# Six gate pairs by seven products instead of four, the first pair loaded and summed ahead of its stage, and the order of the vector work before it

## The reference, cut to what matters

```python
h = x @ p['w_in'][l]
fa, fb, fm = split_cols(h, [A_COLS, B_COLS, 2 * D_MODEL])
...
o_b = o_b.reshape(bsz, t, D_B).astype(x.dtype) * jax.nn.silu(z_b)
g_a, g_b = split_cols(fm, [D_MODEL, D_MODEL])
merged = jax.nn.sigmoid(g_a) * (o_a @ p['w_up_a'][l]) + jax.nn.sigmoid(g_b) * (o_b @ p['w_up_b'][l])
y = layer_norm(ALPHA * x + merged @ p['w_out'][l], p['ln_g'][l], p['ln_b'][l])
```

## Time and profile before

| | us |
|---|---|
| median of 3 runs | 2148.93 |
| lowest and highest of them | 2145.84, 2149.21 |
| profiled execution, its own time | 2150.8 |
| its span from the first to the last instruction | 2149.1 |
| PE busy | 2109.5 (98%) |
| DVE busy | 1081.9 (50%) |
| POOL, ACT busy | 511.9, 411.4 |

### The profile page before, as it was taken

How to read it: one execution, slowest core, us unless ns; L and a number is a source line. 1 busy time by engine, 2 the same in 40 slices (tenths; PEclk the granted TensorE clock), 3 DMA queues, 4 the chain that set the end, 5 groups by cost and what they waited for, 6 DMA issues and landing times.

```text
span 2149.1 us, 48889 instructions
## 1 busy us (share of the span) xinstructions
PE 2109.5 (98%) x21468; PEld 1861.7 (87%) x21468; DVE 1081.9 (50%) x1885; ACT 411.4 (19%) x1168; POOL 511.9 (24%) x380
## 2 busy tenths in 40 slices
PE   9999999999999999999999999999999999999997
PEld 8999977777887779999999999777777877899996
DVE  3454344443725523674575443555547165247745
ACT  1111111122113511110121121222221043111002
POOL 3433300002011123333324333000020112134333
PEclk9999999999999999999999999999999999999998
DMA  8445333335643365555354453332365334645551
GB/s 305 169 160 171 118 133 101 101 101 201 218 138 104 109 228 184 162 167 177 128 182 163 157 172 123 110 101 101 101 218 191 119 118 144 217 170 165 172 170 66
DMA packets 89124, 329.51 MB, mean 153 GB/s; under 512 B 11920, under 2 KB 11936, under 8 KB 86608
## 3 DMA queue, kind: packets, MB, share of 16 engines
q1 hardware_dynamic: 74736, 268.60, 37.1%
q0 software_dynamic: 11872, 53.59, 7.1%
q10 hardware_dynamic: 2304, 4.20, 0.6%
HBM read 315.91 MB, written 18.82 MB: 156 GB/s over the span
## 4 chain that ended last, share of the span: by engine, by line
PE 94%; DVE 4%; DMA 1%; issue 1%; ACT 0%; POOL 0%; SPq 0%; ACTq 0%; POOLq 0%; DVEq 0%
PE PB L805 28%; PE PB L853 3%; PE PB L884 3%; PE PB L880 3%; PE PB L875 3%; PE PB L868 3%; PE PB L864 3%; PE PB L858 3%; PE PB L1288 3%; PE PB L940 1%; PE PB L1022 1%; PE PB L1005 1%; PE PB L1007 1%; PE PB L1000 1%; PE PB L996 1%; PE PB L969 1%
## 5 line engine op out<-in xcount | busy, mean ns | idle before, releaser
L805 PE MATMUL PB<-XT,WT 128*128 128x264 f32 (+1 forms) x2816 | 691.3, 395 | 0.0
L805 PEld LDWEIGHTS PB<-XT,WT 128*128 128x128 f32 (+1 forms) x2816 | 508.5, 189 | 100.4 <-issue 15.2
L1494 ACT ACTIVATE VT<-PB 128x132 f32<-128x132 f32 (+2 forms) x280 | 79.3, 292 | 581.4 <-PE PB L868 130.6
L1494 ACT ACTIVATE ARENA<-PB 128x128 f32<-128x128 f32 (+7 forms) x187 | 76.4, 429 | 261.5 <-PE PB L1187 65.6
L631 POOL DMA_DIRECT2D out<-in_c_win x16 | 8.1, 507 | 460.2 <-DVE ARENA L2113 460.2
L631 POOL DMA_DIRECT2D ARENA<-in_c_sel x64 | 40.0, 625 | 231.2 <-issue 231.2
L652 POOL TENSOR_TENSOR TOEP<-WT 128x1024 f32<-128x1024 f32 x20 | 47.2, 2360 | 172.8 <-PE PB L868 167.8
L652 POOL TENSOR_TENSOR TOEP<-H 128x1024 f32<-128x1024 f32 x20 | 48.2, 2410 | 141.6 <-PE PB L868 137.0
L868 PE MATMUL PB<-ARENA,TOEP 128*128 128x132 f32 x640 | 78.5, 276 | 0.0
L875 PE MATMUL PB<-ARENA,TOEP 128*128 128x132 f32 x640 | 78.5, 276 | 0.0
L884 PE MATMUL PB<-XT,TOEP 128*128 128x132 f32 x640 | 78.5, 276 | 0.0
(11 more groups left out here) (480 smaller groups left out, 4204.4 us busy)
## 6 DMA issues: line engine op xcount, KB each, us to landing
WT<-in_w_all SPq DMA_DIRECT2D x340, 512.0 KB, 4.4
H<-in_w_all SPq DMA_DIRECT2D x120, 512.0 KB, 4.4
KNVC<-in_w_all SPq DMA_DIRECT2D x40, 512.0 KB, 3.9
out<-in_c_win POOLq DMA_DIRECT2D x16, 512.0 KB, 5.3
ARENA<-in_c_cmp POOLq DMA_DIRECT2D x64, 128.0 KB, 4.4
ARENA<-in_c_sel POOLq DMA_DIRECT2D x64, 128.0 KB, 4.0
TOEP<-in_toep POOLq DMA_DIRECT2D x2, 2048.0 KB, 8.6
ARENA<-in_states POOLq DMA_DIRECT2D x4, 1024.0 KB, 11.2
```

Source lines behind the costliest of these rows:

```text
L805: ins = mm(PB[rows, bank, 0:T], WT[:, s, k, 0:rows.stop - rows.start], x, start=start, stop=stop)
L1494: return act(out, in_, ACT.Copy)
```

## The change

Four of the `ga` tiles per layer move from the table of tiles to the pairs: `TILES` has 42 entries and there are six gate pairs. The units behind the second scores go from 36 to 20; one unit is left under `gates`. The four blocks of the first gate pair go to buffers that are free early (the place of the k columns and of the first keys and values in H, and the second half of KNVC), and SP issues their loads ahead of tiles 35, 36, 40 and 37. POOL's first two sums wait for the scaled probabilities (`as_v ps`) instead of `zb_v out`. DVE makes t1 to t4 and OS2 directly behind the value product (`as_t o`), then `back`, OS4 and the z_B products.

```diff
+LAST_GA = 4
-         + [("zb", ZB0 + i) for i in range(8)] + [("gb", i) for i in range(16)] + [("ga", i) for i in range(8)])
+         + [("zb", ZB0 + i) for i in range(8)] + [("gb", i) for i in range(16)] + [("ga", i) for i in range(LAST_GA)])
-GATES, UPS, PAIRS = 4, 8, 8
+GATES, UPS, PAIRS = (16 - LAST_GA) // 2, 8, 8
+FIRST_AT = (35, 36, 40, 37)
-BEHIND_MIX.update({"as0": 12, "as1": 36, "as2": 6, "as3": 3})
+BEHIND_MIX.update({"as0": 12, "as1": 20, "as2": 6, "as3": 3})
...
+        old_keys, old_values = flat(H[:, K0:K0 + 8, :]), flat(H[:, KV0 + 2:KV0 + 6, :])
+        PW_FIRST = [block_of(old_keys, 0), block_of(old_keys, BLK * P), block_of(old_values, 0), PW[0][3]]
+        pair_blocks = lambda g: PW[g % 2] if g else PW_FIRST
...
+            def load_first(L, b):
+                if b == 0:
+                    sp.wait_ge(*step("gn_v", L, "out"))
+                if b == 2:
+                    sp.wait_ge(*step("as_v", L, "q"))
+                    sp.wait_ge(st_kv, 16 * (L + 1))
+                if b == 3:
+                    sp.wait_ge(*step("cm_v", L * 2 + 1, "out"))
+                load_block(L, 0, b)
+
             def load_pairs(L):
-                sp.wait_ge(*step("zb_v", L, "out"))
-                for b in (0, 2, 1, 3):
-                    load_block(L, 0, b)
                 for b in range(4):
                     sp.wait_ge(tile_done[b // 2], (L + 1) * N_TILES // 2)
                     load_block(L, 1, b)
-                for g in range(2, GATES + 2):
+                sp.wait_ge(*step("zb_v", L, "out"))
+                for b in (0, 2, 1, 3):
+                    pair_loaded(sp, L, 0, b)
+                    if b == 3:
+                        sp.wait_ge(*step("gp_t", L * GATES, "st4p"))
+                    load_block(L, 2, b)
+                for g in range(3, GATES + 2):
...
                 elif i > 3:
+                    if i in FIRST_AT:
+                        load_first(L, FIRST_AT.index(i))
                     sp.wait_ge(tile_done[s], u)
...
-                po.wait_ge(*step("zb_v", L, "out"))
+                po.wait_ge(*step("as_v", L, "ps"))
                 pair_loaded(po, L, 0, 0)
                 pair_loaded(po, L, 0, 2)
-                mark("os_p", L * BOTH, add(OS3, PW[0][0], PW[0][2], ALU.subtract), "s3")
+                mark("os_p", L * BOTH, add(OS3, PW_FIRST[0], PW_FIRST[2], ALU.subtract), "s3")
...
-                own("as_t", "tr")
-                for g in range(NG):
...
+                own("as_t", "o")
                 low, high = XT[:, 0:BLK, :], XT[:, BLK:KT, :]
...
                 second_sum(0)
+                own("as_t", "tr")
+                for g in range(NG):
...
+                mark("as_v", L, ins, "back")
                 fourth_sum(0)
+                own("zb_a", "tanh")
+                mark("zb_v", L, stt(TZB[:, :, :], TZB[:, :, :], 1.0, H[:, ZB0:ZB0 + 8, :], ALU.add, ALU.mult), "sz")
+                own("as_v", "back")
+                own("zb_v", "sz")
+                mark("zb_v", L, stt(H[:, ZB0:ZB0 + 8, :], H[:, Q0:Q0 + 8, :], 0.5, TZB[:, :, :], ALU.mult, ALU.mult), "out")
```

More of the change, by code:

```diff
@@ L81 @@
 LAST_ODD, EVENS = MAINS - 1 - MAINS % 2, (MAINS + 1) // 2
-PAIRED = [("ga", i) for i in range(8, 16)] + [("up", i // 2 + i % 2 * 8) for i in range(16)] + [("out", i) for i in range(16)]
-GATES, UPS, PAIRS = 4, 8, 8
+PAIRED = [("ga", i) for i in range(LAST_GA, 16)] + [("up", i // 2 + i % 2 * 8) for i in range(16)] + [("out", i) for i in range(16)]
+GATES, UPS, PAIRS = (16 - LAST_GA) // 2, 8, 8
 OUTS = GATES + UPS
@@ L307, in hybrid_trunk @@
         fresh()
-        TZB = take(P, 8, T)
+        TZB, OS = take(P, 8, T), take(P, 256)
         used[0] = slot
@@ L314, in hybrid_trunk @@
         PTZ = take(P, 4 * NB, 32).rearrange("p (i b) n -> p i b n", b=NB)
-        PCZ, PNT, OS = take(P, NB, 32), take(NB, 2, P), take(P, 256)
+        PCZ, PNT = take(P, NB, 32), take(NB, 2, P)
         assert used[0] <= at_att
@@ L509, in load_block @@
                 done = w_in_slot[b // 2][b % 2] if g % 2 else w_in_pair[b]
-                sp.dma_start(PW[g % 2][b], w_all[L, N_TILES + 2 * MAINS + 2 * g + b // 2, :, BLK * (b % 2):BLK * (b % 2) + BLK, :]).then_inc(done, 16)
+                sp.dma_start(pair_blocks(g)[b], w_all[L, N_TILES + 2 * MAINS + 2 * g + b // 2, :, BLK * (b % 2):BLK * (b % 2) + BLK, :]).then_inc(done, 16)
             def load_main(L, m, b):
@@ L737, in _ @@
                             dma(SVS[odd][:, m, pg, :].rearrange("p (a n) -> p a n", n=P), c_sel[L, page, :, 2:4, :], d_att[odd])
-                po.wait_ge(*step("zb_v", L, "out"))
+                po.wait_ge(*step("as_v", L, "ps"))
                 pair_loaded(po, L, 0, 0)
                 pair_loaded(po, L, 0, 2)
-                mark("os_p", L * BOTH, add(OS3, PW[0][0], PW[0][2], ALU.subtract), "s3")
+                mark("os_p", L * BOTH, add(OS3, PW_FIRST[0], PW_FIRST[2], ALU.subtract), "s3")
                 pair_loaded(po, L, 0, 3)
-                mark("os_p", L * BOTH, add(OS1, PW[0][2], PW[0][3], ALU.add), "s1")
+                mark("os_p", L * BOTH, add(OS1, PW_FIRST[2], PW_FIRST[3], ALU.add), "s1")
                 for g in range(1, BOTH):
@@ L890, in gate_pair @@
                 t0, t1 = slice(0, HALF), slice(HALF, T)
-                w = PW[g % 2]
+                w = pair_blocks(g)
                 first, second = PB[:, 2 + g % 2 * 2, :], PB[:, 3 + g % 2 * 2, :]
@@ L1448, in _ @@
                     elif g:
-                        all_projected(pe, L, "ga", 7)
+                        all_projected(pe, L, "ga", LAST_GA - 1)
                     up_pair(L, g)
@@ L1771, in _ @@
                     sc.wait_ge(*step("gp_v", it, "fin"))
-                    gate = H[:, 8 + 2 * g:10 + 2 * g, :].rearrange("p t n -> p (t n)")
+                    gate = H[:, LAST_GA + 2 * g:LAST_GA + 2 + 2 * g, :].rearrange("p t n -> p (t n)")
                     mark("gp_a", it, act(gate, f, ACT.Tanh, scale=0.5), "tanh")
@@ L2361, in second_sum @@
                     else:
-                        ins = tt(OS2, OS1, PW[g % 2][0], ALU.subtract)
+                        ins = tt(OS2, OS1, pair_blocks(g)[0], ALU.subtract)
                     mark("os_v", L * BOTH + g, ins, "s2")
@@ L2373, in fourth_sum @@
                     else:
-                        ins = tt(OS4, PW[g % 2][1], OS2, ALU.subtract)
+                        ins = tt(OS4, pair_blocks(g)[1], OS2, ALU.subtract)
                     mark("os_v", L * BOTH + g, ins, "s4")
+                own("as_t", "o")
                 low, high = XT[:, 0:BLK, :], XT[:, BLK:KT, :]
@@ L2385, in _ @@
                 second_sum(0)
-                fourth_sum(0)
+                own("as_t", "tr")
+                for g in range(NG):
+                    rows = slice((g % 2) * HD, (g % 2) * HD + HD)
+                    o = PB[rows, 0, (g // 2) * P:(g // 2) * P + P].rearrange("p (b h) -> p b h", h=NH)
+                    ins = cp(hq(g), o[:, :, 4 * g:4 * g + 4].rearrange("p b r -> p r b"))
+                mark("as_v", L, ins, "back")
+                fourth_sum(0)
+                own("zb_a", "tanh")
[3 more added lines that the diff above has]
+                mark("zb_v", L, stt(H[:, ZB0:ZB0 + 8, :], H[:, Q0:Q0 + 8, :], 0.5, TZB[:, :, :], ALU.mult, ALU.mult), "out")
                 def up_tokens(h):
@@ L2462, in _ @@
                     if g == 0:
-                        all_projected(ve, L, "ga", 7)
+                        all_projected(ve, L, "ga", LAST_GA - 1)
                         ve.wait_ge(*step("gp_a", (L + 1) * GATES - 1, "tanh"))
```

## The result

The changed kernel takes 2164.03 us (median of 7 runs, 2161.73 to 2172.26), the kernel before 2149.21 us beside it (7 runs, 2145.84 to 2156.03). The ratio is 1.0061, with an interval of 1.0049 to 1.0074: slower by 13 us (the medians alone lie 14.8 apart). The forecast was 2151.2 us within 2143.5 to 2155.5, so the time lies 8.5 us above the upper end. The profiled executions say the same: the span went from 2149.1 to 2162.4 us, 13.3 more.

The account below looks back on a forecast made before the run. TensorE, busy 98% of the span, was taken to bound the kernel. Per layer -28.6 + 25.2 + 3.8 = +0.4, for both +0.8, plus 1.5 for the clock: +2.3 on 2148.93 gives 2151.2 us, range 2143.5 to 2155.5.

Parts of the forecast that it names:

- Work of PE: Both layers: 64 units fewer against two more gate pairs, so PE's own work falls 3.4 us a layer, 6.8 in all.
- The place of the wait: At the first gate pair's fifth product, line 936, PE waits for VectorE's small addition, line 2441, in each layer.
- The size of the wait: At the first gate pair's fifth product: addition done after 13.25 us, PE there after 9.4, so 3.8 us a layer.
- T0: The end of the samples' value product, 785.41 before the change; the prediction counts PE's and VectorE's times from it.
- The clock: Behind the two waits of 3.8 us: one fall to half clock expected, +1.5 us, between 0 and +3.4.
- The rival on the clock: Behind the waits the clock falls in both layers: waits of 4.1, two half-clock stretches, +4.8 us, 2153.7; chance 0.20.
- signs of being wrong: Line 936 waiting under 2 us, tile 40 or values over a microsecond, or half clock past one stretch a layer.
- The values: Second half of the values: cover down to some 0.4 us, so a slightly later landing makes PE wait 0 to 0.5.
- the scaled probabilities: Line 805, behind the second scores: 20 units end at 768.3, probabilities finished at 764.99; no wait, 3.3 us to spare.
- tile 40: Its first half lands near 756.4, just when PE needs it; wait taken as 0, up to 1 us.
- the pairs behind the first: Gate stage: six gate pairs 12.60 us apart, but for the first.
- The range: Whole kernel: from 2143.5 us, where the wait is merely shorter, to 2155.5, for clock and loads together.

## Why the prediction was wrong

- **Work of PE (-6.8 us): right.** The stretch that holds the change is 6.7 us shorter where nothing waits in it. With at most 0.2 us of waiting left in each gate stage the kernel gains 5.8 us by the medians, and 3.2 to 9.3 by the interval of the ratio (0.15% to 0.43% of 2151.4).
- **The place of the wait: right.** Line 936 waits for line 2441 in both layers, and the two z_B products run right before it.
- **The size of the wait: the step that failed.** The sum of VectorE's instructions from T0 on took "the two large products for z_B, 2.46 and 2.28" from the earlier trace rows, where GpSimd stood idle beside them. In the new order product 4 of the same pair releases GpSimd's sums for pair 1 in the middle of the two products, and the second takes 4.31. The wait is 5.8 instead of 3.8 in each layer, 4.0 us in all; held back, the sums leave 3.86. The prediction looked at GpSimd's first two sums alone, and did not ask where those for pair 1 would fall. The trace of before could have hinted at it: the 128x132 sum of line 2427 takes 0.59 us at 818.33, while a GpSimd sum runs from 816.41 to 818.76; the same form takes 0.28 at its shortest (line 1948).
- The Trainium skill, "SBUF — State Buffer", section "Who interferes with whom", states that only the port pair which VectorE shares with GpSimd causes contention, as an exclusive lock; that a VectorE instruction with two inputs in SBUF contends with a GpSimd instruction that reads SBUF, and one with at most one such input, outside the two-port modes, does not; and that the order of issue decides which one blocks. The trace agrees: the four ends above are 2.20 and 2.21 apart, one instruction at a time, and the addition with one input in PSUM took its usual 0.29 beside a GpSimd sum.
- **The clock (+1.5 us for one fall): too small.** It fell in both layers, for 6.8 us each, and cost 2.9 and 2.0. The price of a fall had been taken from one stretch of 3.4 us, of which half was the upper end. The longer wait may be part of this: after 3.86 us of idling one layer fell, for 3.4 us; after 5.8 both did, for about twice that, in one profiled execution each. The rival on the clock was right in kind, not in size, and one of the prediction's signs of being wrong came true (half clock for longer than one such stretch a layer). This term failed beside the wait: with the wait back at 3.86 the time is still 2157.81, above the upper end.
- **The values (0 to 0.5 us): a little over,** 1.1 in one layer and none in the other. That too is over the microsecond that the prediction named as a sign of being wrong.
- **What held:** the scaled probabilities were there in time at line 805, tile 40 did not stall, and the pairs behind the first lie 12.60 us apart.
- **Two small slips.** The prediction counts eleven instructions between T0 and the addition; the order has twelve, the four copies as four, and the sum has them all. And not all of the vector work was over at 797.65 before: the second weight sum started at 808.22 and the fourth ended at 810.7, 2.2 us ahead of the addition. Neither changes the forecast.
- **The excess as a whole.** The span grew by 13.3 us where 2.3 were forecast. Of the 11.0 between them 4.0 are the wait, 3.4 the clock behind it, 1.1 the values, and 2.5 the rest that fits half clock elsewhere.
- **The range.** Its upper end added clock and loads to a wait of 3.8. No case in it had VectorE's instructions take longer than in their old place.

Not settled: what brings the stretches of half clock outside the gate stage. Runs of one kernel differ by up to 13 us here (2138.97 to 2151.87), and the mean granted clock of these two runs is 0.997 and 0.993.

## What to carry to other kernels

When work moves in time, look up what runs beside it in the new place, and what the work ahead of it will release there on other engines, before taking its duration from the old one. Here it was GpSimd beside VectorE. If an engine in order stands between a released buffer and the next product, put the few short instructions that TensorE asks for first, and the long ones behind them, even if these then take nearly twice as long. A wait of TensorE of several microseconds costs more than itself, since the products after it may run at half clock; price both together.

## What the runs showed of the hardware

- Elementwise instructions on VectorE (with two inputs in SBUF) and on GpSimd, both from SBUF to SBUF, took turns: 2.36 us became 4.31 and 2.41 became 4.46, and a sum of 0.30 us took 2.44.
- The order decides who pays: a GpSimd sum that started 0.33 us ahead of VectorE's product kept its 2.42 us, and VectorE's took 4.31.
- In the profiled executions half clock came in one of two waits of 3.86 us, and in both of 5.8. With matmuls that belong to nothing in the gap it came in neither.
